# Two-block layer kernel: order of tanh, gate additions and one branch tile in the attention steps

## The reference, cut to what matters

```python
proj = h @ w_in                                   # q, k, v of A, B, C, and the gates gl
br_a = stick_breaking(qa, ka, va)                 # sigmoid scores, reverse cumulative product
br_b = forgetting(qb, kb, vb, log_f)              # softmax
br_c = indexed_sparse(qc, kc, vc, qi, ki, wi)     # softmax over selected keys
gates = sigmoid(gl.reshape(b, s, 3, 1024))
y = (gates[:, :, 0] * (br_a @ w_branch[0]) + gates[:, :, 1] * (br_b @ w_branch[1])
     + gates[:, :, 2] * (br_c @ w_branch[2]))
x = x + y @ w_out
x = x + square(relu(rmsnorm(x) @ w_up)) @ w_down
```

## Time and profile before

| | |
|---|---|
| median of 3 runs | 1595.86 us (1595.25 to 1596.62) |
| the profiled execution | 1595.55 us, its span 1593.5 us |
| TensorE busy | 1528.8 us, 96% of the span |
| VectorE, ScalarE, GpSimd busy | 801.8, 336.4, 274.6 us |
| granted TensorE clock, mean | 0.985 of full speed |

### The profile page before, as it was taken

The page is one execution under the profiler, slowest core; times in us unless marked ns, Lnnn a source line. Parts: engine busy times, 40 slices in busy tenths (PEclk is TensorE's granted clock), DMA queues, the critical chain, the costliest instruction groups (busy, mean ns, idle before and its releaser), DMA issues.

```text
span 1593.5 us, 32163 instructions
## 1 busy us (share of the span) xinstructions
PE 1528.8 (96%) x14083; PEld 1344.9 (84%) x14083; DVE 801.8 (50%) x1492; ACT 336.4 (21%) x712; POOL 274.6 (17%) x145
## 2 busy tenths in 40 slices
PE   7999999799799899999999999999999999999998
PEld 2667768688689688998888999998999888899997
DVE  2342334655653326667531866522766753176643
ACT  1102133533432301033400121000104340012000
POOL 3404001000000035762200000003566310000000
PEclk9999999899899999999999999999999999999999
DMA  9322330000002524433334444553443323344551
GB/s 350 113 69 90 107 132 3 2 3 16 5 15 95 134 106 159 159 109 131 132 110 155 159 159 165 183 158 107 159 159 132 134 107 130 134 159 167 182 183 39
DMA packets 110907, 191.68 MB, mean 120 GB/s; under 512 B 20888, under 2 KB 27296, under 8 KB 110640
## 3 DMA queue, kind: packets, MB, share of 16 engines
q1 hardware_dynamic: 109776, 188.29, 34.4%
q0 software_dynamic: 960, 1.33, 0.3%
q10 hardware_dynamic: 32, 0.01, 0.0%
HBM read 188.57 MB, written 1.05 MB: 119 GB/s over the span
## 4 chain that ended last, share of the span: by engine, by line
PE 85%; DVE 4%; PEld 3%; ACT 2%; issue 2%; DMA 2%; DVEq 1%; ACTq 1%; SPq 0%; PEldq 0%
PE psum L1383 22%; PE psum L1242 13%; PE psum L1217 13%; PE psum L939 6%; PE psum L864 4%; PE psum L1493 3%; PE psum L1238 3%; PEld psum L1512 2%; PE psum L1428 2%; PE psum L1100 2%; PE psum L1512 2%; PE psum L1532 1%; DMA arena<-in_x 1%; PE psum L1462 1%; PE psum L1307 1%
## 5 line engine op out<-in xcount | busy, mean ns | idle before, releaser
L1383 PEld LDWEIGHTS psum<-arena 128*128 128x128 f32 x3136 | 350.5, 192 | 0.1
L1383 PE MATMUL psum<-arena 128*128 128x128 f32 x3136 | 350.5, 274 | 0.0
L1242 PEld LDWEIGHTS psum<-arena 128*128 128x128 f32 x2240 | 254.3, 192 | 8.7 <-issue 8.0
L1242 PE MATMUL psum<-arena 128*128 128x128 f32 x2240 | 260.9, 275 | 0.0
L1957 ACT ACTIVATE arena<-psum 128x512 f32<-128x512 f32 (+6 forms) x238 | 116.1, 494 | 646.4 <-PE psum L1383 176.7
L1217 PE MATMUL psum<-arena 128*128 128x256 f32 x928 | 202.6, 379 | 0.0
L1217 PEld LDWEIGHTS psum<-arena 128*128 128x128 f32 x928 | 175.3, 189 | 25.6 <-issue 0.3
L817 POOL TENSOR_TENSOR arena<-arena 128x1024 f32<-128x1024 f32 x12 | 28.2, 2353 | 565.3 <-DMA arena<-in_w_in 516.1
L939 PEld LDWEIGHTS psum<-arena 64*64 64x64 f32 x3072 | 92.3, 134 | 6.6 <-issue 4.4
L939 PE MATMUL psum<-arena 64*64 64x64 f32 x3072 | 96.1, 219 | 1.4 <-issue 1.4
L1512 PE MATMUL psum<-arena 128*128 128x256 f32 x336 | 73.4, 379 | 0.8 <-issue 0.8
(11 more groups left out here) (392 smaller groups left out, 1914.2 us busy)
## 6 DMA issues: line engine op xcount, KB each, us to landing
arena<-in_w_in SPq DMA_DIRECT2D x33, 2048.0 KB, 7.8
arena<-in_w_up SPq DMA_DIRECT2D x16, 2048.0 KB, 8.6
arena<-in_w_down SPq DMA_DIRECT2D x16, 2048.0 KB, 7.9
arena<-in_w_out SPq DMA_DIRECT2D x6, 2048.0 KB, 8.3
arena<-in_w_branch SPq DMA_DIRECT2D x6, 2048.0 KB, 7.6
arena<-in_mod_w SPq DMA_DIRECT2D x5, 2048.0 KB, 14.1
arena<-in_w_in SPq DMA_DIRECT2D x3, 1024.0 KB, 6.0
arena<-in_w_in SPq DMA_DIRECT2D x12, 256.0 KB, 4.7
```

Source lines behind the costliest of these rows:

```text
L1242: mm = pe.matmul(b[:, n * P:(n + 1) * P], left[:, k, n * P:(n + 1) * P], right[:, k, :], start=k == 0, stop=k == half - 1)
L1383: mm = pe.matmul(b[:, n * P:(n + 1) * P], left[:, k, n * P:(n + 1) * P], right[:, k, :], start=first and n == 0 and k == 0, stop=last and ...
```

## The change

Three edits, all in the attention steps of both layers:

1. ScalarE's tanh of a gate chunk in steps 2 to 10 is put behind the two copies of the step (it was between the exponentials or sigmoids and the copies). The last chunk's tanh stays where it was.
2. In the four steps of kind A, VectorE runs `finish(i)` one gate addition sooner: in even steps 6, finish, 7, 5 (was 6, 7, finish, 5), in odd steps 2, finish, 3, 4 (was 2, 3, finish, 4).
3. In step 12 the branch tile br00 is computed between the transposes wT11 and the values o11; the plan deals out its bank there too.

```diff
         if i < len(PAIRS):
             p += [(f"gl{i // 2}_{m}", "D", 1) for m in GATE_STEPS[i % 2][1]]
+        else:
+            p += [("br00", "D", 1)]
         if i:
             p += [(f"o{i - 1}", "A", 1)]
-    p += [(f"br{b}{n}", "D", 1) for b in range(3) for n in range(4)] + [(f"out{n}", "D", 1) for n in range(4)]
+    p += [(f"br{b}{n}", "D", 1) for b in range(3) for n in range(4) if b or n] + [(f"out{n}", "D", 1) for n in range(4)]
...
+            def branch(b_, ns):
+                w = use_chunk(pe, n0 + N_IN + b_, l).rearrange("p k n -> p (k n)").rearrange("p (k n) -> p k n", n=D)
+                ly.wait_emptied(pe, f"o{4 * 'BAC'.index('ABC'[b_]) + 3}", l)
+                for n in ns:
+                    tiles(f"br{b_}{n}", w, (2 * n * P, (2 * n + 1) * P), src=br[:, b_], ks=4)
+
...
                 if i < last:
                     gate_products(GATE_STEPS[i % 2][1])
+                else:
+                    branch(0, range(1))
...
             for b_ in range(3):
-                w = use_chunk(pe, n0 + N_IN + b_, l).rearrange("p k n -> p (k n)").rearrange("p (k n) -> p k n", n=D)
-                ly.wait_emptied(pe, f"o{4 * 'BAC'.index('ABC'[b_]) + 3}", l)
-                for n in range(4):
-                    tiles(f"br{b_}{n}", w, (2 * n * P, (2 * n + 1) * P), src=br[:, b_], ks=4)
+                branch(b_, range(0 if b_ else 1, 4))
...
-                if i and i % 2 == 0 and i < last:
-                    gates_out(i // 2 - 1)
                 if i:
                     weights_out(i - 1)
                 if i == last:
                     gates_out(GATES - 1)
                 if i:
                     values_out(i - 1)
+                if i and i % 2 == 0 and i < last:
+                    gates_out(i // 2 - 1)
...
-                gate_added(i // 2, GATE_STEPS[i % 2][0])
+                ms = GATE_STEPS[i % 2][0]
+                before = len(ms) - 1 if PAIRS[i][0] == "A" else len(ms)
+                gate_added(i // 2, ms[:before])
                 finish(i)
-                gate_added(i // 2, GATE_STEPS[i % 2][1])
+                gate_added(i // 2, ms[before:] + GATE_STEPS[i % 2][1])
```

## The result

The changed kernel takes 1608.2 us (median of 4, 1606.88 to 1609.12), the kernel before 1596.0 us: a ratio of 1.0076, 95% interval 1.006 to 1.0092. It is slower by 12.2 us; the forecast was 1606.4, that is +10.6. Its profiled execution took 1607.49 us. Of the 50 executions of the kernel before that stand beside the experiments, one took 2253 us at a mean granted clock of 0.651; the ratios leave it out.

A forecast was written before the change was run, and what follows sets the result against it. TensorE, busy 96% of the span, bounds the kernel; at most 8.4 us could be won. Per layer: stalls +6.2, removed waits -2.7, clock +1.8, giving +5.3; twice that is +10.6, so 1606.4 us, range 1600 to 1611.

The forecast's parts named there:

- gl2_2 waits for gl2_7's addition: Step 5: first gate product waits for a bank released by an addition now behind `finish`; TensorE 2.0 us late.
- gl3_2 waits for gl3_7's addition, in all: Step 7: first gate product starts 7.85 us late, of which 5.85 us are one new stall.
- transposes of step 7, without the clock: Transposes of step 7 start at 755.7 instead of 749.45, 6.2 us late, their old 1.46 us wait included.
- clock, first / second layer: Step 7's 5.85 us stall lowers TensorE's clock; bounds 0 or 2.05 us, taken as +1.8 us a layer.
- Nothing won by the earlier scans: Steps 4 and 6: `finish` starts up to 1.7 us sooner but waits out GpSimd's sum, ending at 741.65 against 741.66.
- The bank ring: Steps 5 and 7 wait for product 7's banks; odd-step additions free banks needed 9 us or more after filling, costing nothing.
- Old waits: Waits at step 7's transposes (1.46 us) and the values of steps 8, 9, 12 (0.52, 1.21, 0.99 us) all go.
- the 0.52 us are gone: Step 8: with tanh behind the weights copy, the copy ends about 1 us sooner and the values' wait disappears.
- R1: Rival: the clock stays up behind the new stall; +7.0 us, 1602.9; chance 0.15.
- R2: Rival: `finish` escapes GpSimd in even steps, new stalls shrink to about 0.3 us; 3.6 us a layer gained, 1588.7; chance 0.08.
- R3: Rival: bank wait costs little, such as VectorE forestalling a GpSimd sum; -0.9 us a layer, 1594.1; chance 0.07.
- R4: Rival: step 9's 1.21 us stay or a new wait arises beside GpSimd's sums; up to +2.2 a layer, 1610.8; chance 0.10.

The follow-up runs named there:

- experiment 4: Changed kernel with GpSimd's sums of chunks 3 and 4 started only after finish(4) and finish(6); ratio 0.9981 to the kernel before, median 1592.87 us.
- 1: Changed kernel without edit 2 (edits 1 and 3 alone, VectorE's old order); ratio 0.9997 to the kernel before, median 1594.57 us.
- 3: Changed kernel with edit 2 kept in odd steps alone, old VectorE order in steps 4 and 6; ratio 0.998 to the kernel before, median 1592.6 us.
- 5: Kernel before with edit 1 alone (tanh behind the copies); ratio 1.0019, median 1598.34 us.
- experiment 2: Kernel before with edit 2 alone (`finish` moved); ratio 1.007, median 1605.47 us.
- experiment 7: Kernel before with only GpSimd's sums of chunks 3 and 4 started after finish(4) and finish(6); ratio 1.0025, median 1598.72 us.
- 6: Edits 1 and 3, VectorE's old order, and step 9's weights copy ahead of its exponentials; ratio 0.9966 to the kernel before, median 1589.63 us.
- 8: Edits 1 and 3, GpSimd's sums later, weights copies ahead of the exponentials in steps 8 and 9; ratio 0.9955 to the kernel before, median 1588.07 us.

## Why the prediction was right

Its time, sign and mechanism held; two terms were mis-sized, in opposite ways, and that the total came within 2 us is in part luck: the first layer came out 0.7 us under its forecast, the second 2.1 over it. Terms for the first layer, each as TensorE's distance from its start of step 4, after minus before:

| Step of the prediction | forecast | measured |
|---|---|---|
| gl2_2 waits for gl2_7's addition | +2.0 | 12.45 - 10.51 = +1.94 |
| gl3_2 waits for gl3_7's addition, in all | +7.85 | 35.76 - 28.04 = +7.72 |
| transposes of step 7, without the clock | +6.2 | 41.21 - 33.34 - 1.77 = +6.10 |
| clock, first / second layer | +1.8 / +1.8 | +1.77 / +1.62 + 2.89 = +4.51 |
| waits of steps 8, 9, 12, and restarts | -2.7 | -3.27 |
| a layer | +5.3 / +5.3 | +4.6 / +7.4 |

**Nothing won by the earlier scans.** Right, and shown from both sides: beside the sums the first instruction takes 2.6 us, without them 0.96 (experiment 4). Five contended two-input instructions, two in step 6 and one in step 4 of the changed kernel and two in step 7 of experiment 4, all end 0.81 or 0.82 us behind the end of the sum beside them. This is the exclusive lock of the Trainium skill (SBUF — State Buffer, "Who interferes with whom"); these rows agree with it.

**The bank ring.** Right. The profile names the addition of product 7 as the releaser in both stalls, and each disappears with the old order (1, 3) and nearly so when that addition comes early enough (4). In odd steps the prediction gave it "9 us or more after the filling" and so no cost. That was too much room. In the kernel before, gl2_3 was filled at 726.62 + 3.84 = 730.46, and gl3_6, on the same bank, at 738.44, after 1.95 us of multiplying: TensorE wanted the bank back some 6 us after filling it. It cost nothing in the changed kernel, where TensorE itself was late (gl3_3 was added by 759.82, gl4_6 wanted near 761.8); on its own it cost 0.4 us a layer (3), and with the sums moved 1.63 us (4).

**Old waits.** All four went, as forecast. The step that failed in size is "-0.52 - 1.21 - 0.99": a wait also costs something beyond the idle time in brackets. Behind the 1.46 us the gate product began 0.90 us after the transposes and not 0.66, and took 0.10 us longer: 0.35 us. At each of the other three it is 0.07 us, by which an instruction that need not wait starts ahead of the recorded end of the one before. They sum to the missing 0.55 us.

**Edit 1.** The prediction says of it that "the 0.52 us are gone". In the changed kernel they are, since VectorE had room. Alone it wins nothing (5): the exponentials of step 9 don't depend on TensorE.

**The clock.** The step that failed in size is "clock +1.8" in the second layer. The long stall cost 2.89 us there, above the bound of 2.05, and the 1.86 us stall, for which I had charged nothing, cost 1.62. The bound was half of one case's return. By the windows the clock was at half for about 6.8 us around both long stalls, 747.2 to 754.0 and 1272.8 to 1279.7, and what costs is the part behind the restart. In the first layer it fell 2.6 us after TensorE fell idle, in the second only 5.0 us after, so 3.7 us of it came behind the restart in the one and 6.1 in the other; half of that is 1.9 and 3.05 us, an estimate, beside 1.77 and 2.89 measured. (The restart at 550.76, on which the bound rests, is the first product of the first layer, after first_block and not in it.) R1 (the clock stays up) is out: behind all four 5.7 us stalls of the changed kernel and experiment 2 the clock was low, for losses of 1.77, 2.89, 1.79 and 1.50 us. R2 and R3 needed `finish` to escape GpSimd, which it did only when the sums were moved; R4 would have needed a wait in step 9, and there was none.

Outside the stretch the profiled executions differ by -1.6 us ahead of the first layer's step 4 and by +1.65 us between the two layers, which cancel: 4.6 + 7.4 - 1.6 + 1.65 = 12.05 of the 12.1 us between the spans. Neither is in edited work (last section).

## What to carry to other kernels

Before an instruction is moved behind a long one, list what it releases, not only what it needs: here a 0.42 us addition freed a PSUM bank that TensorE wanted back 4.0 us after filling it. In the kernel before, gl3_7 was filled when this row's wait ended, at 740.15, and gl3_2 began on its bank at 744.15, while `finish` beside GpSimd's sums took 8.7 us:
```profile
740.15 0.42 DVE L2661 TENSOR_TENSOR arena<-psum,arena 128x256 f32<-128x256 f32 x1 [1.29 <-PE psum L1242]
```
If two engines are released by the same event and exclude one another, as here, starting the one that loses sooner wins nothing; moving the other away does, if it has a better place (4), and not if it only stands in the way elsewhere (7). And a wait is worth its length only if the next one downstream hangs on it too: of two waits in a row that hang on another engine's chain, removing the first lengthens the second.

## What the runs showed of the hardware that was not expected

**Short stalls sometimes lower the clock.** Of TensorE's stalls of 1.8 to 1.9 us in these steps, in the changed kernel and experiments 1, 2 and 5, two of eight were followed by the low clock: the second layer of the changed kernel (32 matmuls in 5.46 us instead of 3.84) and the first of experiment 1. Of the two stalls of 2.93 us in experiment 7, the one in the first layer was, and the one in the second was not. What decides it stays open; none of these runs varied it.

**The clock also falls while TensorE is busy.** Before, in the second layer, TensorE timeline and windows (us, PE busy, clock, DMA share, GB/s):
```profile
1106.69 3.63 PE L1225 MATMUL psum<-arena 128*128 128x4 f32 x32
1110.18 5.35 PE L1260 MATMUL psum<-arena 128*72 128x256 f32 x16
```
```profile
1110.00:1112.00 2.00, 2.00 (x10) 0.80 0.00 0
1112.00:1114.00 2.00, 2.00 (x7) 0.50 0.00 0
```
TensorE had no idle time, but its last work before the fall was 3.6 us of matmuls of 4 columns. In the changed kernel's profiled execution the same place was at half clock for about 6.8 us (1112.0 to 1120.0: 0.61, 0.50, 0.50, 0.69) instead of 3.4, which is the +1.65 us above. It does not fall there always: in experiments 1, 5, 6 and 8 it was low for 3.4 us as before, in 2, 3, 4 and 7 not at all. Between the end of the first layer's stretch and step 4 of the second the ten profiled executions have 433.7, 435.3 or 437.0 us, in step with that. The prediction had overlooked this fall when it said that each came in a sparser stretch.

**What varies between these kernels ahead of step 4 lies in first_block.** From TensorE's restart at the head of the first layer (550.76 before) to step 4 all ten profiled executions take 165.34 to 165.37 us. What differs is when that restart comes, and the clock of the first 60 us goes with it. Where its mean was 0.97, TensorE entered step 4 at 714.2 to 714.5 us (the changed kernel, 3 and 8); where it was 0.94, at 715.7 to 716.8 (before, 1, 2 and 4); where it was 0.91, at 717.6 and 718.7 (6 and 5). Experiment 7 is the exception, 718.8 with 0.94, and in its profile the clock was low for another 3.4 us at 485 to 490 us. Differences of 2 us between kernels on this chip have to be read from the changed stretch, not from one execution's time.
